# A two-layer diffusion transformer step on one core: the first norm of each layer per token, its modulation in four rows of five ticks, and VectorE alone scaling h

## The reference, cut to what matters

```python
def rms_norm(x, g):
    xf = x * lax.rsqrt(jnp.mean(x * x, axis=-1, keepdims=True) + EPS)
    return xf * g

def adaln(cond, w, b):                       # w is (1024, 6144) in each layer
    return jnp.split(jax.nn.silu(cond) @ w + b, 6, axis=-1)

sh1, sc1, g1, sh2, sc2, g2 = mod
h = rms_norm(x, p['norm1']) * (1 + sc1) + sh1
... = jnp.split(h @ p['w_in'], ...)          # ten groups of columns; mla_cq (256) is projected first
```

## Time and profile before

| | us |
|---|---|
| Three runs of the kernel before | 1734.14, 1739.01, 1741.87 (median 1739.01) |
| The profiled execution, its own time | 1741.36 |
| Its span in the trace | 1739.1 |
| Busy in it: PE, DVE, ACT, POOL | 1610.1, 949.3, 664.1, 148.3 |

### The profile page before, as it was taken

How to read it: one execution, slowest core, us unless ns; L and a number is a source line. 1 busy time by engine, 2 the same in 40 slices (tenths; PEclk the granted TensorE clock), 3 DMA queues, 4 the chain that set the end, 5 groups by cost and what they waited for, 6 DMA issues and landing times.

```text
span 1739.1 us, 28317 instructions
## 1 busy us (share of the span) xinstructions
PE 1610.1 (93%) x11686; PEld 1489.9 (86%) x11686; DVE 949.3 (55%) x1480; ACT 664.1 (38%) x1045; POOL 148.3 (9%) x107
## 2 busy tenths in 40 slices
PE   5878897899999999999988799978999999999998
PEld 3755895589999999999967569946999999999998
DVE  3653346856555545654584433497566456554553
ACT  4554533753422322232244454357433222332231
POOL 1002102520000000000010030064000000000000
PEclk9898998999999999999999899989999999999999
DMA  9440443311222222223534205341222222222211
GB/s 312 156 144 1 72 142 103 112 47 52 76 94 70 69 81 73 73 73 116 191 106 135 85 1 119 106 155 50 73 74 73 73 73 73 73 73 73 91 55 61
DMA packets 150856, 160.14 MB, mean 92 GB/s; under 512 B 16390, under 2 KB 132808, under 8 KB 150728
## 3 DMA queue, kind: packets, MB, share of 16 engines
q1 hardware_dynamic: 150024, 158.13, 29.7%
q10 hardware_dynamic: 576, 0.16, 0.0%
q0 software_dynamic: 128, 0.05, 0.0%
HBM read 153.41 MB, written 4.65 MB: 91 GB/s over the span
## 4 chain that ended last, share of the span: by engine, by line
PE 78%; DVE 11%; ACT 6%; issue 3%; DMA 1%; ACTq 0%; DVEq 0%; SPq 0%
PE ps L1552 33%; PE ps L1895 26%; PE ps L1645 10%; PE ps L1617 2%; PE ps L1669 2%; PE ps L1532 1%; DVE extrema L1306 1%; PE ps L1578 1%; ACT pt_c L788 1%; DVE extrema L1289 1%; PE ps L1722 1%; PE ps L1700 1%; DMA ada_own<-in_w_ada 1%; DVE mod L1147 1%; DVE w_lo L1134 1%
## 5 line engine op out<-in xcount | busy, mean ns | idle before, releaser
L788 ACT ACTIVATE w_hi<-w_raw 128x2048 fp32r<-128x2048 f32 (+1 forms) x90 | 169.9, 1887 | 333.8 <-PE ps L1552 324.3
L1348 DVE SCALAR_TENSOR_TENSOR xT<-ps,mod,xT 128x128 f32<-128x128 f32 (+2 forms) x432 | 190.0, 440 | 195.8 <-PE ps L1552 183.9
L1134 DVE TENSOR_TENSOR w_lo<-w_raw,w_hi 128x2048 fp32r<-128x2048 f32 (+1 forms) x90 | 203.1, 2257 | 140.4 <-ACT w_hi L788 138.9
L1895 PE MATMUL ps<-xa_hi,w_hi 128*128 128x320 f32 (+1 forms) x1024 | 236.1, 312 | 0.0
L1895 PE MATMUL ps<-xa_lo,w_hi 128*128 128x320 f32 (+1 forms) x1024 | 235.2, 311 | 0.0
L1895 PE MATMUL ps<-xa_hi,w_lo 128*128 128x320 f32 (+1 forms) x1024 | 235.1, 311 | 0.0
L1552 PE MATMUL ps<-z_hi,w_hi 128*128 128x320 f32 x1024 | 233.7, 310 | 0.9 <-DVE xT L1348 0.9
L1552 PE MATMUL ps<-z_lo,w_hi 128*128 128x320 f32 x1024 | 233.4, 309 | 0.0
L1552 PE MATMUL ps<-z_hi,w_lo 128*128 128x320 f32 x1024 | 233.3, 309 | 0.0
L1106 ACT ACTIVATE z_relu<-z_relu,sink_shift 128x128 f32<-128x128 f32 (+1 forms) x128 | 72.2, 564 | 307.0 <-DVE z_relu L1452 304.9
L1895 PEld LDWEIGHTS ps<-xa_hi,w_hi 128*128 128x128 f32 x1024 | 173.5, 189 | 0.3
(11 more groups left out here) (241 smaller groups left out, 2364.4 us busy)
## 6 DMA issues: line engine op xcount, KB each, us to landing
w_raw<-in_mlp_w SPq DMA_DIRECT2D x64, 1024.0 KB, 5.2
ada_own<-in_w_ada SPq DMA_DIRECT2D x54, 512.0 KB, 4.5
w_raw<-in_w_in SPq DMA_DIRECT2D x14, 1024.0 KB, 7.8
ada_mix<-in_w_ada SPq DMA_DIRECT2D x21, 512.0 KB, 7.8
ada_room<-in_w_ada SPq DMA_DIRECT2D x15, 512.0 KB, 8.9
w_raw<-in_w_out SPq DMA_DIRECT2D x8, 768.0 KB, 5.3
ada_first<-in_w_ada SPq DMA_DIRECT2D x6, 512.0 KB, 9.1
x_in<-in_x_sample SPq DMA_DIRECT2D x1, 2048.0 KB, 8.6
```

The source lines that it names most:

```text
L788: do(nc.scalar.activation(out, in_, ACT.Copy), sem)
L1134: do(V.tensor_tensor(w_lo[:, n % 2, 0:w], w_raw[:, n % 2, 0:w], f32(w_hi[:, n % 2, 0:w]), ALU.subtract), w_lo_ready)
L1348: do(V.scalar_tensor_tensor(dst, src, gate[:, m:m + 1], dst, ALU.mult, ALU.add), sem if last else None)
L1895: last = M.matmul(bank(b + a_, s1 - s0), w[r][:, k, c:c + P], x[:, k, s0:s1], start=k == 0 and q == 0, stop=k == KC - 1 and q == 2)
```

## The change

The squares of layer 0 are taken per token: ScalarE squares x_in (tokens on partitions, 1024 channels) and its accumulator gives 128x5 sums. In layer 1 TensorE sums over channels into columns (`token_sums`). Mean, root and reciprocal work on 128x5, and TensorE spreads the result over all partitions (`spread_rstd`), from where ScalarE copies it (`take_rstd`). VectorE takes the transposed x from PSUM in place of ScalarE. The modulation groups come in the order scale, shift (first halves), scale, shift (second halves), each four units and a turn: 20 ticks in rows of five. The first row and the spread stand before h, the others between its chunks on ScalarE and VectorE; `project_cq` on TensorE is cut after chunk 0 in layer 0 and whole in layer 1. VectorE takes over GpSimd's multiplications. Weights 0 are loaded after the eighth ada unit. The first block of ckv goes ahead of the late ticks. GpSimd's waits for rpb_dma stay, and ScalarE has one more.

```diff
+ADA_GROUPS = (2, 0, 3, 1)
-CQ_BANKS = (0, 1, 3, 7, 2)
+CQ_BANKS = (4, 5, 0, 6, 7)
...
+        for q in range(4):
+            FIRST_TICKS += [(None, ("unit", 4 * q + k)) for k in range(4)] + [(("turn", q), None)]
+        def ada_acc_bank(first, k):
+            return (2, 1)[k // 4 % 2] if first % 48 == 0 else ada_banks(first)[0]
...
 SyncE
-            load_adas(0, range(AFTER_X))
-
-            sp.wait_ge(t_done, KC)
+            load_adas(0, range(8))
+            load_weights(0)
+            load_adas(0, range(8, AFTER_X))
+
+            sp.wait_ge(t_done, trans_ix.at[("x", KC - 1)] + 1)
+            sp.wait_ge(x_squared, NT)
             load_adas(0, range(AFTER_X, 16))
-            load_weights(0)
+            load_weights(1)
...
-            load_weights(1)
 GpSimd
-            def scale_x(nrm):
...
-                        do(pool.tensor_tensor(hf[:, c % 4, :], xT[:, c, :], rstds[0][:, :], ALU.mult), hf_pool)
...
-                scale_x(2 * l)
 ScalarE
+            def take_rstd(l):
+                i = acc_ix.at[(l, "rstd")]
+                act.wait_ge(m_done, i + 1)
+                do(nc.scalar.activation(rstds[0][:, :].rearrange("p (a n) -> p a n", a=2), acc_view(i), ACT.Copy), m_act)
+            def first_norm(l):
+                if l:
+                    load_sqrt()
+                    for c in range(KC):
+                        act.wait_ge(y_read, (l * GROUPS - 1) * KC + c + 1)
+                        square_x(2 * l, c)
+                    ada_ticks(48 * l, range(5))
+                    root_x(2 * l)
+                    take_rstd(l)
+                    ada_ticks(48 * l, range(5, 10))
+                else:
+                    root_x(0)
+                    ada_ticks(0, range(5))
+                    take_rstd(0)
+                    ada_ticks(0, range(5, 10))
+                    split_hi(0)
+                h_halves(2 * l, range(1))
+                ada_ticks(48 * l, range(10, 15))
+                h_halves(2 * l, range(1, 2))
+                ada_ticks(48 * l, range(15, 20))
+                h_halves(2 * l, range(2, KC))
...
-                act.wait_ge(acol_ready, nrm + 1)
                 for c in chunks:
+                    act.wait_ge(acol_ready, 3 * l + 1 + c // 4)
+                    act.wait_ge(mod_ready, 12 * l + 2 + 2 * (c // 4))
+                    act.wait_ge(hf_ready, KC * l + c + 1)
...
-            for c in range(KC):
-                act.wait_ge(t_done, c + 1)
-                copy(xT[:, c, :], trans_view(c, NTOK), t_act)
+            def square_tokens(t):
+                do(nc.scalar.activation(x_sq[:, :], x_in[:, t, :], ACT.Square, accum_out=tok_rstd[:, t:t + 1]), x_squared)
+            act.wait_ge(x_in_dma, 32)
+            square_tokens(0)
+            square_tokens(1)
...
-            for c in range(KC):
-                square_x(0, c)
-            ada_ticks(0, range(8))
+            for t in range(2, NT):
+                square_tokens(t)
             load_sqrt()
 VectorE
             def h_of(l):
+                dve.wait_ge(m_act, acc_ix.last_reader(acc_ix.at[(l, "rstd")])[1])
                 for c in range(KC):
+                    if c == 2:
+                        ada_ticks(48 * l, range(5, 10))
+                        if l == 0:
+                            split_lo(0)
+                    if c == 4:
+                        ada_ticks(48 * l, range(10, 15))
+                        scales(nrm, 4, 4)
+                    if c == 6:
+                        ada_ticks(48 * l, range(15, 20))
                     if c in H_DVE:
...
+                    else:
+                        do(V.tensor_tensor(hf[:, c % 4, :], xT[:, c, :], rstd[:, :], ALU.mult), hf_ready)
                     if c >= 2:
                         lo(c - 2)
...
+            def take_x(c):
+                i = trans_ix.at[("x", c)]
+                dve.wait_ge(t_done, i + 1)
+                do(V.tensor_copy(xT[:, c, :], trans_view(i, NTOK)), t_dve)
+            for c in range(4):
+                take_x(c)
...
+                mean(2 * l)
                 if l:
-                    mean(2 * l)
-                    ada_ticks(48 * l, range(6))
-                    invert(2 * l)
-                    ada_ticks(48 * l, range(6, 18))
+                    ada_ticks(48 * l, range(5))
+                    scales(2 * l, 0, 4)
+                invert(2 * l)
+                if l == 0:
+                    ada_ticks(0, range(5))
+                    scales(0, 0, 4)
                 h_of(l)
+                dve.wait_ge(const_dma, 64)
 TensorE
+            def token_sums(l, part):
+                out = bank(acc_banks(acc_ix.at[(l, "sum1")]), 2 * NT)
+                x, ready, count = ((rstds[0], sum_used, (KC - 2) * 2 * l), (sq[:, (KC - 1) % 2], sq_ready, KC * 2 * l))[part]
+                pe.wait_ge(ready, count)
+                for t in range(NT):
+                    at0 = NT * part + t
+                    last = M.matmul(out[:, at0:at0 + 1], x[:, P * t:P * t + P], ones[:, 0:1], start=True, stop=True,
+                                    skip_group_check=True)
+            def spread_rstd(l):
+                pe.wait_ge(tok_ready, l + 1)
+                for t in range(NT):
+                    for s, e in ((P * t, P * t + P),) if t != 2 else ((P * t, HALF), (HALF, P * t + P)):
+                        last = M.matmul(bank(b + s // HALF)[:, s % HALF:s % HALF + e - s],
+                                        tok_rstd[:, t:t + 1].broadcast_to([P, P]), ident[:, s - P * t:e - P * t],
+                                        start=True, stop=True, skip_group_check=True)
+            def first_norm(l):
+                wait_read(trans_ix, did["t"] - 1, t_act, t_dve)
+                wait_read(trans_ix, did["t"] - 2, t_act, t_dve)
+                if l:
+                    ada_ticks(48 * l, range(4))
+                    begin_acc((l, "sum1"))
+                    token_sums(l, 0)
+                    token_sums(l, 1)
+                    ada_ticks(48 * l, range(4, 7))
+                    pe.wait_ge(y_read, did["y"])
+                    spread_rstd(l)
+                    ada_ticks(48 * l, range(7, 20))
+                    project_cq(l, 45 * l, range(KC))
+                else:
+                    ada_ticks(0, range(4))
+                    spread_rstd(0)
+                    ada_ticks(0, range(4, 15))
+                    project_cq(0, 0, range(1))
+                    ada_ticks(0, range(15, 20))
+                    project_cq(0, 0, range(1, KC))
...
+                project(l, U + 1, "ckv", range(1))
+                pe.wait_ge(p_read, proj_at[(l, "cq", NT - 1)] + 1)
+                pe.wait_ge(ada_reduced, 12 * l + 4)
                 ada_ticks(late, late_ticks(l, 1))
-                project(l, U + 1, "ckv")
+                project(l, U + 1, "ckv", range(1, NT))
```

More of the change, by code:

```diff
@@ L810, in ada_tick @@
                         act.wait_ge(ada_turned, u // 4)
-                    copy(ada_row[:, :], bank(ada_banks(first)[0]), ada_rows)
+                    copy(ada_row[:, :], bank(ada_acc_bank(first, unit[1])), ada_rows)
             def ada_ticks(first, ks):
@@ L1170, in invert, with scales @@
             def invert(nrm):
-                rstd = rstds[nrm % 2]
+                rstd = rstds[1][:, :] if nrm % 2 else tok_rstd
                 dve.wait_ge(sqrt_ready, nrm + 1)
-                do(V.reciprocal(rstd[:, :], rstd[:, :]), rstd_ready)
-            def scales(nrm):
+                do(V.reciprocal(rstd, rstd), None if nrm % 2 else tok_ready)
+            def scales(nrm, c=0, n=KC):
                 l, which = nrm // 2, nrm % 2
-                sc = (SCALE1, SCALE2)[which]
-                gain = vcol[:, l, (R_N1, R_N2)[which]:(R_N1, R_N2)[which] + KC].unsqueeze(2).broadcast_to([P, KC, 2])
-                do(V.scalar_tensor_tensor(acol[:, :, :], mod[:, l % 2, sc:sc + KC, :], 1.0, gain, ALU.add, ALU.mult),
+                sc, g = (SCALE1, SCALE2)[which] + c, (R_N1, R_N2)[which] + c
+                do(V.scalar_tensor_tensor(acol[:, c:c + n, :], mod[:, l % 2, sc:sc + n, :], 1.0,
+                                          vcol[:, l, g:g + n].unsqueeze(2).broadcast_to([P, n, 2]), ALU.add, ALU.mult),
                    acol_ready)
@@ L1572, in ada_tick @@
                     if u % 4 == 0 and u:
-                        pe.wait_ge(ada_rows, u // 4)
+                        pe.wait_ge(ada_rows, u // 4 - (first % 48 == 0 and unit[1] >= 4))
                         if b_acc == b_turn and unit[1]:
                             pe.wait_ge(ada_reduced, u // 4)
-                    c = 512 * b_acc + AC * (u % 4 // 2)
+                    c = 512 * ada_acc_bank(first, unit[1]) + AC * (u % 4 // 2)
                     for j in range(AR):
@@ L1592, in sums @@
                 out = acc_view(acc_ix.at[(l, which)])
-                for x, ready, count in ((rstd[:, :], sum_used, (KC - 2) * (nrm + 1)),
-                                        (sq[:, (KC - 1) % 2, :], sq_ready, KC * (nrm + 1))):
```

(2 more changed lines are left out.)

153 lines of the change are left out of this document (66 added, 87 removed).

## The result

| | us |
|---|---|
| Kernel before, 6 runs | median 1737.97 (1734.14 to 1741.87) |
| Changed kernel, 6 runs | median 1726.76 (1722.82 to 1731.13) |
| Ratio, 95% interval | 0.9937, 0.9921 to 0.9954 |
| The profiled execution after, and its span | 1722.82, 1720.9 |

The change is 0.6% faster. The forecast was 1720.0 and -19.0; the medians give -11.2. The time lies in the range of 1712 to 1731, but the sum was some 8 us too large, and the two profiles hide that: their spans, 1739.1 and 1720.9, differ by 18.2.

A forecast was written before the change was run, and what follows sets the result against it. TensorE held 78% of the span, so time is won where it waits, at both layers' starts: -13.5 in layer 0 and -5.5 in layer 1 give -19.0, 1720.0 from a median of 1739.01; range 1712 to 1731.

The forecast's parts named there:

- the hinge: Layer 0, row four: TensorE's chunks 1 to 7 and ScalarE's h_hi 2 to 7 stand behind unit 15, in at 37.1.
- Behind it: Layer 0 after cq: late units land near 57, TensorE waits about 0.5; ckv covers the norm's delay of 2.
- signs of being wrong: Layer 0's cq ending after 60, TensorE waiting over 2 us for late units, or first attention under 10 us earlier.
- Start of layer 1: Earlier norm and row order end layer 1's cq 4.6 earlier at the old clocks, 7.0 at full clock; -5.5 taken.
- hidden under ScalarE and TensorE: GpSimd's four multiplications moved to VectorE cost 3.4 in all, covered by other engines; cover called thin.
- the first rival: Clock stays low through layer 0's cq: -6.6 in layer 0, -12 in all, 1727; chance 0.12.
- The loads rival: Unit 15 or the late units slip by 4, and all of layer 0 with them: 1724; chance 0.10.
- set the first attention: Rival: gains, caches, pool weights or a load set it; layer 0 gives 2, layer 1 4.6: 1732; chance 0.09.
- slower: Rival: the clock does not rise in cq nor in what follows, up to 1759; chance 0.05.

The follow-up runs named there:

- the repeat: The changed kernel timed and profiled again with no edit: 1726.07, ratio 0.993 to the kernel before.
- all three edits: Changed kernel with layer 0's cq uncut, ckv's block 0 without its wait, VectorE's fourth reduction earlier; run twice: 1720.77 (0.9903) and 1719.99 (0.9898).
- ckv's block free: Changed kernel with block 0 of ckv no longer waiting for four of cq's five banks to be read: 1725.75 (0.9932).
- the one with dummies: Kernel uncut, ckv's block unwaiting, reduction earlier, plus six unused matmuls before each of attention C's first three pairs, both layers: 1716.79 (0.9868).

## Why the prediction was right, and where it was not

*Start of layer 0: -14.0 forecast for cq's end, -10.5 and -9.6 measured.* The step that failed is the hinge, "Unit 15 at 37.1". That figure was bytes over 348 GB/s, counted from x's arrival. The first unit already landed at 13.0, where this gives 11.5, and another 1.0 was lost between units 9 and 10: unit 15 landed at 39.6, in the repeat at 38.3. Why the loads came late no run shows. The second part was the chunk ahead of it. The sum has chunk 0 of cq from 32.5 to 35.7, out of the way before unit 15. But unit 11, "in at 31.1" there, landed at 33.6, and h_lo 0 was ready at 35.9 in place of 32.5, so chunk 0 ran from 36.1 to 39.1, at the lower clock, with the matmuls of units 12 to 15 all behind it. ScalarE's copy came at 41.14 in place of 37.6 or so, of which 2.5 are the landing and most of the other 1.0 the chunk (1.1 and 2.0 in the repeat). Everything behind it moved by the same 3.5. This 3.5 is the whole of the miss; the steps after the hinge held, 16.2 from the copy to cq's end against 16.3 (ScalarE's list, its pause for the shift of the second half, TensorE following h_lo).

*Behind it.* ckv's block 0 was costed at nothing. Its wait for a copy takes 0.7, and up to the first exponents another 0.9 is lost (0.1 in the repeat), so -10.5 arrives as -8.9. I had -13.5. One of the forecast's own signs of being wrong thus came true: the first attention starts 8.9 earlier (8.8 in the repeat), and not 10.

*Start of layer 1: -5.5 forecast, -4.75 at cq's end, -4.1 behind ckv and -3.2 at the first exponents (-4.8 in the repeat).* Mechanism and size held, at the low end of 4.6 to 7.0; TensorE kept PEclk 1.00 through cq. I took the clock to be the uncertain part. It was the pause of 1.5 for the reduction of row four, of which 0.7 counts, that kept it low; it was in my list.

*GpSimd.* "hidden under ScalarE and TensorE" may be true of what VectorE took over (no run tests it alone) and is beside the point: the multiplications' price before lay in what they held up. I wrote that an add took 1.50 beside them and put the silence into the numbers, so the sum is right, but I never priced it as a part. It is the largest: 4.0 + 5.6 us of the new order's gain hang on it by the stages, 6 by the medians. No run takes back the norm per token or the order of the rows alone, so their shares are not shown.

*What I did not foresee:* the output projection's +1.5 per layer. The sum by stages without attention C, then: -8.9 - 3.2 + 3.0 = -9.1, and in the repeat -8.8 - 4.8 + 3.0 = -10.6, against medians of -11.2 and -9.2.

*The rivals.* The clock stayed at the lower level for chunk 0 and had risen by chunk 1, so the first rival did not come about where I put it (cq's 105 matmuls ran at 0.12). The start of attention C is nearer to it, where groups of matmuls between waits stand at PEclk 0.50. The rule of the Trainium skill ("TensorE: Matmul & The Clock Gate", section "HAM oscillation — how this bites in real kernels") has every next group of matmuls behind a wait start at the lower level. The trace agrees from 965 to 974 in layer 1 and not behind it, where PEclk is 1.00 up to C's end (1012). The loads rival, 4 later, was the nearest to what happened: 1724, and 3.5 of its 4 came, 2.5 by the landing. The late units did not set the first attention (TensorE takes them at 60.81 without a wait), and the kernel was not slower.

*Luck.* That the range held rests on its width. The profiled 1722.82 is 0.4 from the 1722.4 I had for the profiled execution, because 8.8 gained in attention C stand in for 4.6 missing in layer 0, 2.3 in layer 1 and 3.0 lost in the projections.

## What to carry to other kernels

Give a transfer's landing its own row, not bytes over bandwidth, and look at what stands behind a waiting instruction in its engine's list: moved weights put cq's end 11 us later because of the list. When two engines block each other, price the blocking as well as the work; and expect nothing of removing it where another engine ends the wait (here the same edit was worth nothing in one order and 6 us by the medians in the other). And when a stage gets shorter, check that its first mark did not move, and what the stages beside it did. Before comparing two profiles, check stages that the change does not touch: here they carried half of the difference.

## What the runs showed of the hardware that I had not expected

The granted clock differs between executions of one program at the same place: near its start attention C stands at 0.50 for 3 us in one profile (125 to 128 in layer 0, all three edits) and for 23 in another (968 to 991, ckv's block free), and its stage took 44.4 to 50.8. Six small matmuls ahead of each of three pairs brought the clock to 0.93 and 1.00 there and the stage to 43; how much of the 3 to 4 us off the whole is theirs is open.

The output projection began at the lower level in both profiles of the changed kernel in both layers, with the same instructions and the same pause ahead of it as before. Over all profiles it is neither tied to one kernel nor to a long or short C stage: the kernel with ckv's block free had long C stages and a fast projection in both layers, the one with dummies short ones and a fast projection. Why is left open; no run was aimed at it.

One multiplication of 128x640 on GpSimd, 1.6 long, held up VectorE's instructions by 1.3 to 1.4, however short they were: a gain of 0.17 as much as scaled halves of 0.58.
